# A hand-written side queue for two attentions: its clock, its rotations and its banks

## The chip, the core and the metric

The kernel runs on one core of a Trainium2 chip. The metric is the device time of one execution in microseconds, lower is better. A run's time is the median of several executions; a profile is taken from one execution more.

## What is computed

Two transformer blocks follow each other on one sequence of 256 tokens and width 1024, in fp32. The change touches the second one, cut here to what matters:

```python
def second_block(x, ...):                       # two layers
    # layer 0: differential attention, 8 heads of 2 x 64, values of 128
    q, k, v = split(rms_norm(h) @ w_qkv)
    q, k = rope(q), rope(k)                     # rotation by position
    p = softmax(causal(q @ k.T * 64 ** -0.5))   # two maps per head
    a = p[:, 0] - lam * p[:, 1]
    h = h + (rms_norm(a @ v, subln_g) * (1 - lambda_init)) @ w_o
    h = h + square(relu(rms_norm(h) @ w_up)) @ w_down
    # layer 1: latent attention, 8 heads, 128 plain and 64 rotated
    c, k_rope = split(rms_norm(h, kv_in_norm_g) @ w_dkv)     # 256 and 64
    k_nope, v = split(rms_norm(c, kv_norm_g) @ w_ukv)
    q_nope, q_rope = split(rms_norm(rms_norm(h) @ w_dq) @ w_uq)
    s = (q_nope @ k_nope.T + rope(q_rope) @ rope(k_rope).T) * 192 ** -0.5
    h = h + (softmax(causal(s)) @ v) @ w_o
    h = h + square(relu(rms_norm(h) @ w_up)) @ w_down
    return rms_norm(h)
```

## The kernel before

All weights come as one stream of units of 128x1024, in an order written out by hand (`stream_plan`). For each unit ScalarE casts a high part (`whi`, L358) and VectorE subtracts it for a low part (`wlo`, L359); five such slots exist, and `feed` casts the next unit as soon as the matmuls of an old one have been issued. Every product with a weight is three matmuls (high by high, low by high, high by low). Each engine runs its queue in program order, waits on semaphores, and the program is written out in Python, so the order of the Python calls is the order in each queue.

PSUM has eight banks: four that rotate (`psum`) and four (`pacc`, called `fix`) that accumulate the wide products. `banks.take()` hands out the next free one, whose next user waits for what freed it. While the attentions run, `fix` joins the rotating four; before the output product starts, `banks.retire(fix)` takes the four back as each comes free.

The attentions run beside a stream of projections. Class `Side` is the queue for this: parts (Python generators) stand in it, `add` enters one with a condition, and `nudge`, called between groups of projection matmuls, moves a clock on and advances at most two parts: an active one that is due, or a new one that may begin. What a part yields is the time until it is due again.

Differential attention: 16 blocks of `qk`, by head a query's block (g = 0) and a key's (g = 8), 24 matmuls each, with a nudge in the middle and one at the end. After a block ScalarE copies it into one of the two `sg` buffers (`roped`, L1469) and POOL multiplies by the cosine (L1470). The rotation (`rope_end`: two fp32 matmuls on TensorE, then L1474 and L1480, or L1474 and L1478 for a key, on VectorE) is a part of the side queue. `diff_head` is a head in four steps: masks and scores, row maxima (`softmax_exp`, L1189, VectorE), exponentials (L1194, ScalarE), normalising (L1529 to L1537, VectorE); transposes (L1167); product with the values, its squares, POOL's power and the scaling (L1551, VectorE); transposes (L1558) and the high and low part for the next product (`chunk_parts`, L585 and L586). A head may start when its query and key are `ripe`: rotated, and at least 2 of the queue's clock old. `rows_times` then multiplies the heads' outputs by `o_a`, with a nudge every half unit.

Latent attention: after the feed-forward part, `cross.finish` turns the rows and casts units, `cross.norms` and two diagonals follow, then the low-rank units run in the order `dkv` (2), `dq` (4), `dkr`, `ukn` (2), `ukv` (2), `uq` (5). `low_norm` normalises the latent rows (L534, POOL's power, L542), `turn` transposes them on TensorE (L562) and `part_scaled` writes their parts. The copies of the keys are L1303 and L1304. The loop over `UQ_ORDER` makes a rotated query block for two heads and then the two heads' plain query blocks, three products each, and `latent_head` is a head in three steps, beside it.

Of the kernel before, what the change touches and what calls it, by code (L numbers as in the profile page):

```python
# [108 lines left out]
class Lane:  # L109


    def __init__(self, engine, sem):
        self.engine, self.sem = engine, sem
        self.count, self.seen = 0, {}
# [63 lines left out]
class Side:  # L178


    def __init__(self, width, gap=2):
        self.width, self.gap, self.now = width, gap, 0
        self.waiting, self.active = [], []
# [5 lines left out]
    def advance(self, part):  # L189

        gap = next(part, self)
        if gap is not self:
            self.active.append((self.now + (gap or self.gap), part))
            self.active.sort(key=lambda entry: entry[0])

    def soon(self, part):

        self.active.insert(0, (self.now + 1, part))

# [8 lines left out]

    def nudge(self):

        self.now += 1
        for _ in range(2):
            if self.active and self.active[0][0] <= self.now:
                self.advance(self.active.pop(0)[1])
            elif len(self.active) >= self.width or not self.begin():
                return
# [11 lines left out]
def build(nc, stream, x, c_row, cols, const, g_post, rel, lam, final_g, out):  # L228
    plan = stream_plan()
    with ExitStack() as ctx:  # L230
# [1109 lines left out]
        born = {}  # L1340

        def ripe(*js):
            return all(j in t_q and side.now - born[j] >= 2 for j in js)

# [171 lines left out]
        def diff_head(hh):  # L1516
# [22 lines left out]
            rooms.give(x1, *ts)  # L1539
            yield 4  # L1540
            pt, t = transpose_p(x0, ts)
            yield
            b, tk = times_v(pt, [vd[:, i, P * hh:P * hh + P] for i in range(2)], P, t, t_v)
# [10 lines left out]
            rooms.give(ds, t)  # L1554
            yield 4
            b = banks.take()
# [4 lines left out]

        side = Side(5)
        born.clear()
        for hh in range(8):
            side.add(diff_head(hh), lambda hh=hh: ripe(hh, 8 + hh))

        def rope_end(at, rope):
            t_q[at], born[at] = next(rope), side.now
            yield

        for hh in range(8):
            for g in (0, 8):
                if hh == 7:
                    banks.retire(fix if g == 0 else [])
                b = banks.take()
                u = Unit(("qk", g + hh))
                tk = block_T(b.ap[:, 0:T], u, range(8), n1, b.free, side.nudge)
                u.release(tk)
                rope = roped(kT[:, hh, :] if g else qT[:, 2 * hh:2 * hh + 2, :], b, tk, 1.0 if g else 0.125, *by_r)
                next(rope)  # L1580
                feed()
                side.nudge()
                side.soon(rope_end(g + hh, rope))
        while banks.leaving:
            side.step()
        cross = Whole([(n1, lambda c: col("mlp_g", c), None, list)])
        rows_times([("o_a", k) for k in range(8)], range(8), n2, None, cross, side.nudge)
        cross.finish()
# [12 lines left out]
        feed_forward("mlp0_", DFF2 // P, False, n1, cross, norms_later(was))  # L1601
        cross.finish(True, 1)
        cross.norms()
# [5 lines left out]
        feed()  # L1609

        widths_kv, acc_of = {"dkv": (n1, 4, T, 0), "dq": (n2, 2, 384, 2)}, {}

# [16 lines left out]
        for name, f, last in [("dkv", f, 1) for f in range(2)] + [("dq", f, 3) for f in range(4)]:  # L1629
            u = Unit((name, f))  # L1630
            for i in range(2):
                low(name, f, u, i, last)
            u.release(pe.last())
            feed()
            if (name, f) == ("dq", 1):
                by_r = scaled_tables(t_diag, 11264)
            if (name, f) == ("dkv", 1):
                t_ckv = low_norm([acc_of["dkv", i] for i in range(2)], fix[0:2], T, 0)
        done_q = [acc_of["dq", i] for i in range(2)]
        ckv, cq = Parts(hhi, hlo), Parts(mhi, mlo)  # L1640
        part_scaled(turn(tmp[:, :, 0:T], 2, t_ckv), [(ckv, lambda c: col("kv_g", c))])
        t_cq = low_norm(done_q, fix[2:4], 384, 512)
# [10 lines left out]
        for f in range(2):  # L1653
            u = Unit(("ukn", f))
            for g in range(4):
                b = banks.take()
                tk = block_T(b.ap[:, 0:T], u, (2 * g, 2 * g + 1), ckv, b.free)
                n = 4 * f + g
                if n == 1:
                    t_kr = next(rope)  # L1660
                t = copied(kn[:, n, :], b.ap[:, 0:T], n, tk)
                banks.give(b, t)
                t_kn.append(t)
            u.release(tk)
            feed()
# [13 lines left out]
        def latent_head(hh):  # L1679
# [12 lines left out]
            for i in range(2):  # L1692
                a, w = widths(i)
                t = dve.do(lambda e: e.tensor_scalar(ex.ap[:, a:a + w], ex.ap[:, a:a + w], rs[:, i:i + 1], None,
                                                     ALU.mult), t)
            yield 3
            pt, t = transpose_p(ex, t)
            yield
            b = banks.take()
# [6 lines left out]
        o2 = Parts(nhi, nlo)  # L1706
        side = Side(5, 2)
        born.clear()
# [3 lines left out]
        for n, blk in enumerate(UQ_ORDER):  # L1712
# [3 lines left out]
            for k in range(3):  # L1716
                m = 3 * n + k
                if m % 8 == 0:
                    units.append(Unit(("uq", m // 8)))
                u = units[m // 8]  # L1720
                w = (m % 8) * P
                tk = products([(b.ap[:, 0:T], [(u.part(w, w + P), cq.rows(k), cq.t[k])], k == 0, k == 2)],
                              [*u.ready, *b.free])
                if m % 8 == 7 or m == 35:
                    u.release(tk)
                    feed()
                if k == 1:
                    side.nudge()
            if blk < 8:
                born[8 + blk], t_qr[8 + blk] = side.now, []  # L1730
                t_qn[blk] = t = (act.do(lambda e: e.activation(qn[:, blk, :], b.ap[:, 0:T], ACT.Copy, scale=scale), tk)
                                 if blk % 2 else
                                 dve.do(lambda e: e.tensor_scalar(qn[:, blk, :], b.ap[:, 0:T], scale, None, ALU.mult), tk))
                banks.give(b, t)
                if pend is not None:
                    t_qr[pend[0]], born[pend[0]] = next(pend[1]), side.now
                    pend = None
            else:
                rope = roped(qr[:, 2 * (blk - 8):2 * (blk - 8) + 2, :], b, tk, scale)
                next(rope)  # L1740
                pend = (blk - 8, rope)
            side.nudge()
        while banks.leaving:
# [4 lines left out]
        cross = Whole([(n1, lambda c: col("mlp_g", 8 + c), None, list)])  # L1748
        rows_times([("o_b", k) for k in range(8)], range(8), o2, None, cross, side.nudge)
        t_fg = sp.load(fg, bass.AP(tensor=final_g.tensor, offset=final_g.offset, ap=[[0, P], [1, D]]), s_fg, 16,  # L1750
# [143 lines left out]
```

How the kernel before makes its waits and increments, by code:

```python
    def wait(self, *after):  # L116
        for a in after:
            for sem, value in ([a] if isinstance(a, tuple) else a or []):
                if self.seen.get(id(sem), 0) < value:
                    self.seen[id(sem)] = value
                    self.engine.wait_ge(sem, value)
# [1 line left out]
    def do(self, op, *after):  # L124
        self.wait(*after)
        self.count += 1
        op(self.engine).then_inc(self.sem, 1)
        return self.sem, self.count
# [6 lines left out]
    def load(self, out, in_, sem, value, *after):  # L136
        self.wait(*after)
        self.engine.dma_start(out, in_).then_inc(sem, 16)
        return sem, value
```

## Time and profile before

| | us |
|---|---|
| median of 3 runs | 1203.94 (1201.38 to 1204.03) |
| the profiled execution's own time | 1204.62 |
| its span, first to last instruction | 1203.3 |
| TensorE busy with matmuls | 1147.3 (95%) |
| VectorE busy | 804.2 (67%) |
| ScalarE busy | 620.8 (52%) |

A matmul is pipelined, and its end is modelled, so a share of TensorE near 100% does not say that it runs at its peak. The mean granted clock is 0.989 of full speed (2.4 GHz). The differential heads run from about 628 to 711 us of the span, the low-rank stage from 912 to 949, the latent heads from 952 to 1001.

### The profile page before, as it was taken

The numbers are of one execution on the slowest core, as the hardware profiler recorded it, in microseconds if no ns is written. First come the engines' busy times: TensorE is split into PE (matmuls) and PEld (weight loads), VectorE is DVE, ScalarE is ACT, GpSimd is POOL, SyncE is SP. The second block draws the span as 40 slices with busy tenths as digits, with TensorE's granted clock in tenths as the row PEclk, the third lists the DMA queues.
The fourth block names the chain that finished last, engine by engine and source line by source line (L and its number), as shares of the span: only waits on it lengthen the run. The fifth ranks groups of instructions, "written<-read, shape, count | busy, mean of one in ns | idle before, by whom it ended". The sixth has DMA issues, their size and how long they took to land.

```text
span 1203.3 us, 19170 instructions
## 1 busy us (share of the span) xinstructions
PE 1147.3 (95%) x7554; PEld 1049.8 (87%) x7554; DVE 804.2 (67%) x1332; ACT 620.8 (52%) x1138; POOL 51.5 (4%) x71
## 2 busy tenths in 40 slices
PE   4999999899999899999999799999998889999997
PEld 4988899699988899999889789999998778999996
DVE  4878888787765665655778766655657665655655
ACT  5645444646655544444555445545446444645543
POOL 3100000000000000000012100000000100000000
PEclk8999999999999899999999999999999999999999
DMA  8969998373322566564453334555554413655530
GB/s 341 401 261 415 354 338 324 141 284 139 106 76 101 197 213 225 202 230 157 159 180 106 106 105 154 197 178 197 186 178 141 171 36 126 241 178 195 188 140 36
DMA packets 34009, 231.75 MB, mean 193 GB/s; under 512 B 3704, under 2 KB 5120, under 8 KB 6528
## 3 DMA queue, kind: packets, MB, share of 16 engines
q1 hardware_dynamic: 31952, 226.24, 51.4%
q10 hardware_dynamic: 1968, 4.29, 1.0%
q8 instruction: 60, 0.98, 0.3%
q14 instruction: 29, 0.24, 0.1%
HBM read 229.45 MB, written 1.06 MB: 192 GB/s over the span
## 4 chain that ended last, share of the span: by engine, by line
PE 78%; DVE 11%; ACT 7%; issue 2%; DMA 1%; POOL 1%; DVEq 0%; SPq 0%; ACTq 0%; POOLq 0%
PE ps L396 36%; PE pacc L396 33%; DVE wlo L359 4%; ACT whi L358 2%; PE ps L406 2%; PE ps L409 2%; ACT wk L1194 2%; PE pacc L406 1%; ACT arena L675 1%; DVE st L1189 1%; POOL st L525 1%; DMA raw<-in_stream 1%; DMA cst<-in_const 1%; PE pacc L409 1%; DVE raw L336 0%
## 5 line engine op out<-in xcount | busy, mean ns | idle before, releaser
L359 DVE TENSOR_TENSOR wlo<-raw,whi 128x1024 fp32r<-128x1024 f32 x353 | 429.4, 1224 | 169.1 <-ACT whi L358 161.6
L358 ACT ACTIVATE whi<-raw 128x1024 fp32r<-128x1024 f32 x353 | 368.5, 1055 | 153.7 <-PE pacc L396 74.3
L396 PE MATMUL ps<-nhi,whi 128*128 128x256 f32 x1256 | 363.8, 290 | 3.3 <-DVE arena L1474 1.8
L396 PE MATMUL ps<-nlo,whi 128*128 128x256 f32 x1256 | 358.1, 285 | 0.0
L396 PE MATMUL ps<-nhi,wlo 128*128 128x256 f32 x1256 | 357.9, 285 | 0.0
L396 PEld LDWEIGHTS ps<-nhi,whi 128*128 128x128 f32 x1256 | 243.3, 194 | 9.2 <-DVE arena L1474 2.0
L396 PEld LDWEIGHTS ps<-nlo,whi 128*128 128x128 f32 x1256 | 243.4, 194 | 4.4 <-issue 0.5
L396 PEld LDWEIGHTS ps<-nhi,wlo 128*128 128x128 f32 x1256 | 243.3, 194 | 0.0
L915 ACT ACTIVATE sg<-ps 128x256 f32<-128x256 f32 x104 | 39.8, 383 | 161.2 <-PE ps L396 161.2
L396 PE MATMUL pacc<-whi,mhi 128*128 128x512 f32 x240 | 95.6, 398 | 0.0
L396 PE MATMUL pacc<-wlo,mhi 128*128 128x512 f32 x240 | 94.0, 392 | 0.0
L396 PE MATMUL pacc<-whi,mlo 128*128 128x512 f32 x240 | 93.5, 390 | 0.0
L917 DVE TENSOR_TENSOR hm<-sg,ps 128x256 f32<-128x256 f32 x104 | 43.7, 420 | 70.7 <-ACT sg L915 70.7
L336 DVE SCALAR_TENSOR_TENSOR raw<-raw,silu_c 128x1024 f32<-128x1024 f32 x72 | 88.2, 1233 | 0.0
L396 PE MATMUL pacc<-whi,hhi 128*128 128x512 f32 x188 | 73.9, 393 | 0.7 <-DVE hm L917 0.7
L396 PE MATMUL pacc<-wlo,hhi 128*128 128x512 f32 x188 | 73.6, 391 | 0.0
L396 PE MATMUL pacc<-whi,hlo 128*128 128x512 f32 x188 | 73.2, 389 | 0.0
L525 POOL TENSOR_TENSOR st<-st,mod 128x1 f32<-128x1 f32 (+1 forms) x36 | 22.7, 631 | 1014.6 <-DVE st L680 598.1
L396 PE MATMUL pacc<-whi,nhi 128*128 128x512 f32 (+1 forms) x128 | 49.6, 388 | 6.8 <-DVE nlo L776 3.4
L396 PEld LDWEIGHTS pacc<-whi,mlo 128*128 128x128 f32 x240 | 45.1, 188 | 9.9
L396 PEld LDWEIGHTS pacc<-whi,mhi 128*128 128x128 f32 x240 | 45.3, 189 | 8.2 <-issue 0.5
L396 PEld LDWEIGHTS pacc<-wlo,mhi 128*128 128x128 f32 x240 | 45.3, 189 | 7.7 <-issue 0.5
(333 smaller groups left out, 1769.9 us busy)
## 6 DMA issues: line engine op xcount, KB each, us to landing
raw<-in_stream SPq DMA_DIRECT2D x213, 1024.0 KB, 4.9
gates<-in_g_post ACTq DMA_DIRECT2D x3, 512.0 KB, 7.2
h<-in_x SPq DMA_DIRECT2D x1, 1024.0 KB, 7.0
cst<-in_const ACTq DMA_DIRECT2D x1, 1024.0 KB, 5.0
arena<-bias_rows ACTq DMA_DIRECT2D x1, 1024.0 KB, 14.0
out<-tmp SPq DMA_DIRECT2D x4, 256.0 KB, 2.2
silu_c<-in_c_row ACTq DMA_DIRECT2D x1, 512.0 KB, 5.7
arena<-in_final_g SPq DMA_DIRECT2D x1, 512.0 KB, 3.4
```

Source lines behind the costliest of these rows:

```text
L336: t = dve.do(lambda e: e.scalar_tensor_tensor(src, src, 1.0, silu_c[:, :], ALU.mult, ALU.mult, accum_out=adac[:, 8 * m + k:8 * m + k + 1]) ...
L358: t_hi = act.do(lambda e: e.activation(whi[:, s, :], src, ACT.Copy), arrived, room)
L359: t_lo = dve.do(lambda e: e.tensor_tensor(wlo[:, s, :], src, whi[:, s, :].bitcast(F32), ALU.subtract), arrived, room, t_hi)
L396: return e.matmul(o, lt[a], rh[b], start=start and first, stop=stop and last)
L406: pe.quiet(lambda e: e.matmul(o, lt, rh, start=start, stop=stop), *after)
L409: return pe.do(lambda e: e.matmul(o, lt, rh, start=start, stop=True), *after)
L525: return pool.do(lambda e: e.tensor_tensor(r, v, ex, ALU.pow), t, t_zero)
L675: return act.do(lambda e: e.activation(junk, src, ACT.Square, scale=D ** -0.5, accum_out=sums[:, f:f + 1]), *after)
L915: t = act.do(lambda e: e.activation(sg[:, m, :], up if gate is None else gate, ACT.Relu if gate is None else ACT.Silu), tk)
L917: t = dve.do(lambda e: e.tensor_tensor(hm[:, m, :], sg[:, m, :], up, ALU.mult), t)
L1189: t = dve.do(lambda e: e.tensor_reduce(mx[:, i:i + 1], src[:, a:a + w], AX_X, ALU.max, negate=True), t_src)
L1194: toks.append(act.do(lambda e: e.activation(dst.ap[:, a:a + w], src[:, a:a + w], ACT.Exp, bias=mx[:, i:i + 1], accum_out=sm[:, i:i + 1]), ...
```

## The change

- The side queue's clock counts microseconds of stream: a nudge moves it by 1.4 beside a half block (0.72 and 0.36 in the latent loop, where it was 1), and every advanced part adds `cost` = 0.8. The heads' yields change with it: 8, 3 and 5 for 4, 2 and 4 in `diff_head`, 5 and 2.5 for 3 and 2 in `latent_head`. `ripe` asks for 2 there and 2.5 here.
- A rotation is no longer put at the head of the queue with a due time one nudge on, but sorted in with 2.8; and its generator ends at once, where before it stayed for one empty step. In the latent loop the rotation is done after the second product of the second plain block, and no longer after the first plain block.
- At the last differential head the four `fix` banks leave two and two.
- `cross.finish` casts two units ahead of the norms instead of one. The transposes and parts of the latent `ckv` stand after the second `dq` unit, and the tables of the rotation after the third; before, the tables stood after the second and the transposes behind the fourth.
- Two blocks of `ukn` share a bank and one copy.

```diff
@@ class Side
-    def __init__(self, width, gap=2):
+    def __init__(self, width, gap=2, cost=0):
...
         gap = next(part, self)
+        self.now += self.cost
         if gap is not self:
...
-    def soon(self, part):
-        self.active.insert(0, (self.now + 1, part))
+    def soon(self, part, gap):
+        self.active.append((self.now + gap, part))
+        self.active.sort(key=lambda entry: entry[0])
...
-    def nudge(self):
-        self.now += 1
+    def nudge(self, time=1):
+        self.now += time
@@ ripe
+        rest = [2]
         def ripe(*js):
-            return all(j in t_q and side.now - born[j] >= 2 for j in js)
+            return all(j in t_q and side.now - born[j] >= rest[0] for j in js)
@@ diff_head
-            yield 4
+            yield 8
             pt, t = transpose_p(x0, ts)
-            yield
+            yield 3
...
-            yield 4
+            yield 5
@@ the differential loop
-        side = Side(5)
+        side = Side(5, 3, 0.8)
+        def nudge():
+            side.nudge(1.4)
         def rope_end(at, rope):
             t_q[at], born[at] = next(rope), side.now
+            return
             yield
...
                 if hh == 7:
-                    banks.retire(fix if g == 0 else [])
+                    banks.retire(fix[2:4] if g else fix[0:2])
...
-                side.nudge()
-                side.soon(rope_end(g + hh, rope))
+                nudge()
+                side.soon(rope_end(g + hh, rope), 2.8)
@@ the low-rank stage
-        cross.finish(True, 1)
+        cross.finish(True, 2)
...
-            if (name, f) == ("dq", 1):
-                by_r = scaled_tables(t_diag, 11264)
             if (name, f) == ("dkv", 1):
                 t_ckv = low_norm([acc_of["dkv", i] for i in range(2)], fix[0:2], T, 0)
+            if (name, f) == ("dq", 1):
+                part_scaled(turn(tmp[:, :, 0:T], 2, t_ckv), [(ckv, lambda c: col("kv_g", c))])
+            if (name, f) == ("dq", 2):
+                by_r = scaled_tables(t_diag, 11264)
-        part_scaled(turn(tmp[:, :, 0:T], 2, t_ckv), [(ckv, lambda c: col("kv_g", c))])
...
-            for g in range(4):
+            for g in range(2):
                 b = banks.take()
-                tk = block_T(b.ap[:, 0:T], u, (2 * g, 2 * g + 1), ckv, b.free)
+                for c in range(2):
+                    k = 4 * g + 2 * c
+                    tk = block_T(b.ap[:, c * T:(c + 1) * T], u, (k, k + 1), ckv, b.free)
...
-                t = copied(kn[:, n, :], b.ap[:, 0:T], n, tk)
+                t = copied(kn[:, n:n + 2, :], b.ap.rearrange("p (c t) -> p c t", c=2), g, tk)
@@ latent_head
-            yield 3
+            yield 5
             pt, t = transpose_p(ex, t)
-            yield
+            yield 2.5
@@ the latent loop
-        side = Side(5, 2)
+        side = Side(5, 2, 0.8)
+        rest[0] = 2.5
...
                 if k == 1:
-                    side.nudge()
+                    if pend is not None and blk % 2 and blk < 8:
+                        t_qr[pend[0]], born[pend[0]] = next(pend[1]), side.now
+                        pend = None
+                    side.nudge(0.72)
...
-                if pend is not None:
-                    t_qr[pend[0]], born[pend[0]] = next(pend[1]), side.now
-                    pend = None
...
-            side.nudge()
+            side.nudge(0.36)
```

## Rows read from the trace of the kernel before

**Rows 1.** Stages between starts of row maxima (us, each engine's busy, clock, DMA, GB/s).
```profile
631.34:640.39 9.05, 9.05 (x71) 8.84 (x70) 7.65 (x19) 4.76 (x13) 1.86 (x2) 1.00 0.32 118
640.39:651.09 10.70, 10.70 (x84) 10.43 (x83) 8.49 (x23) 5.17 (x17) 2.15 (x3) 1.00 0.30 100
...
662.07:673.12 11.05, 9.97 (x76) 9.23 (x74) 8.85 (x24) 5.53 (x18) 2.12 (x3) 1.00 0.26 95
673.12:684.09 10.97, 9.49 (x69) 8.55 (x67) 8.77 (x24) 5.53 (x18) 2.17 (x3) 1.00 0.27 96
684.09:698.22 14.13, 10.23 (x51) 9.44 (x52) 8.95 (x24) 5.53 (x18) 2.14 (x3) 0.76 0.23 76
698.22:706.21 7.99, 7.99 (x43) 6.62 (x42) 5.88 (x20) 3.77 (x14) 0.69 (x1) 1.00 0.38 131
```

**Rows 2.** VectorE's timeline over one head: start, duration, instruction, idle time before it.
```profile
662.07 1.15 DVE L1189 TENSOR_REDUCE st<-ps 128x1 f32<-128x128 f32 x4
...
664.54 0.17 DVE L1530 RECIPROCAL st<-st 128x2 f32<-128x2 f32 x1 [0.64 <-ACT wk L1194]
...
666.82 0.42 DVE L1474 TENSOR_TENSOR arena<-pacc,arena 128x256 f32<-128x256 f32 x1
...
667.61 1.22 DVE L359 TENSOR_TENSOR wlo<-raw,whi 128x1024 fp32r<-128x1024 f32 x1
668.75 0.48 DVE L586 SCALAR_TENSOR_TENSOR n2lo<-pacc,mod,n2hi 128x256 fp32r<-128x256 f32 x1
...
670.10 0.61 DVE L1551 TENSOR_SCALAR wk<-pacc,st 128x128 f32<-128x128 f32 x2 [0.80 <-POOL st L525]
670.63 0.41 DVE L1474 TENSOR_TENSOR sg<-ps,arena 128x256 f32<-128x256 f32 x1
...
671.98 1.23 DVE L359 TENSOR_TENSOR wlo<-raw,whi 128x1024 fp32r<-128x1024 f32 x1
```

**Rows 3.** Timeline of all engines at one head of the latent attention.
```profile
975.10 0.87 DVE L1480 TENSOR_TENSOR arena<-sg,hm 64x256 f32<-64x256 f32 x2
...
976.12 0.46 PE L406 MATMUL pacc<-arena 128*128 128x128 f32 x2 [0.41 <-DVE arena L1480]
...
977.05 0.62 DVE L1189 TENSOR_REDUCE st<-pacc 128x1 f32<-128x128 f32 x2 [0.62 <-PE pacc L409]
```

**Rows 4.** ScalarE's timeline at one block of the differential attention.
```profile
678.75 0.39 ACT L1469 ACTIVATE sg<-ps 128x256 f32<-128x256 f32 x1 [1.16 <-DVE arena L1478]
679.03 1.05 ACT L358 ACTIVATE whi<-raw 128x1024 fp32r<-128x1024 f32 x1
```

**Rows 5.** Stages with TensorE's waits, same columns as the first group.
```profile
683.57:689.31 5.74, 1.32 (x10) 0.95 (x9) 4.44 (x14) 3.82 (x15) 0.73 (x1) 0.94 0.56 186
689.31:695.44 6.13, 6.13 (x26) 5.95 (x27) 3.88 (x9) 0.00 (x0) 0.69 (x1) 0.50 0.00 1
918.64:943.78 25.14, 20.25 (x138) 19.03 (x137) 19.07 (x35) 16.44 (x33) 4.01 (x7) 1.00 0.60 211
949.33:988.70 39.37, 34.42 (x222) 29.33 (x221) 25.34 (x60) 17.83 (x50) 3.20 (x4) 1.00 0.24 81
```

**Rows 6.** TensorE's timeline, one wait and the last head's scores.
```profile
685.79 0.41 PE L1558 MATMUL ps<-cst,wk 128*128 128x128 f32 x2 [2.22 <-ACT wk L1194]
...
704.31 0.60 PE L409 MATMUL ps<-arena 128*128 128x256 f32 x2
```

**Rows 7.** TensorE's timeline in the low-rank stage, matmuls after a wait.
```profile
919.49 0.41 PE L396 MATMUL pacc<-whi,n2hi 128*128 128x384 f32 x1 [0.69 <-DVE wlo L359]
...
923.09 0.41 PE L396 MATMUL pacc<-whi,n2hi 128*128 128x384 f32 x1 [1.25 <-DVE wlo L359]
...
934.51 0.35 PE L396 MATMUL ps<-hhi,whi 128*128 128x256 f32 x1 [1.13 <-DVE hlo L586]
...
938.98 0.39 PE L396 MATMUL ps<-hhi,whi 128*128 128x256 f32 x1 [1.60 <-DVE arena L1304]
```

**Rows 8.** VectorE's timeline in the low-rank stage, the normalised latents.
```profile
928.29 0.48 DVE L542 TENSOR_SCALAR tmp<-pacc,st 128x256 f32<-128x256 f32 x1 [0.66 <-POOL st L525]
```

More of the change, by code:

```diff
@@ L178 @@
 class Side:
-    def __init__(self, width, gap=2):
-        self.width, self.gap, self.now = width, gap, 0
+    def __init__(self, width, gap=2, cost=0):
+        self.width, self.gap, self.cost, self.now = width, gap, cost, 0
         self.waiting, self.active = [], []
@@ L1568, in rope_end @@
             t_q[at], born[at] = next(rope), side.now
+            return
             yield
+        rest[0] = 2
         for hh in range(8):
@@ L1573, in build @@
                 if hh == 7:
-                    banks.retire(fix if g == 0 else [])
+                    banks.retire(fix[2:4] if g else fix[0:2])
                 b = banks.take()
                 u = Unit(("qk", g + hh))
-                tk = block_T(b.ap[:, 0:T], u, range(8), n1, b.free, side.nudge)
+                tk = block_T(b.ap[:, 0:T], u, range(8), n1, b.free, nudge)
                 u.release(tk)
@@ L1586, in build @@
         cross = Whole([(n1, lambda c: col("mlp_g", c), None, list)])
-        rows_times([("o_a", k) for k in range(8)], range(8), n2, None, cross, side.nudge)
+        rows_times([("o_a", k) for k in range(8)], range(8), n2, None, cross, nudge)
         cross.finish()
@@ L1609, in build @@
         feed()
+        ckv, cq = Parts(hhi, hlo), Parts(mhi, mlo)
         widths_kv, acc_of = {"dkv": (n1, 4, T, 0), "dq": (n2, 2, 384, 2)}, {}
@@ L1634, in build @@
             feed()
-            if (name, f) == ("dq", 1):
-                by_r = scaled_tables(t_diag, 11264)
             if (name, f) == ("dkv", 1):
                 t_ckv = low_norm([acc_of["dkv", i] for i in range(2)], fix[0:2], T, 0)
+            if (name, f) == ("dq", 1):
+                part_scaled(turn(tmp[:, :, 0:T], 2, t_ckv), [(ckv, lambda c: col("kv_g", c))])
+            if (name, f) == ("dq", 2):
+                by_r = scaled_tables(t_diag, 11264)
         done_q = [acc_of["dq", i] for i in range(2)]
-        ckv, cq = Parts(hhi, hlo), Parts(mhi, mlo)
-        part_scaled(turn(tmp[:, :, 0:T], 2, t_ckv), [(ckv, lambda c: col("kv_g", c))])
         t_cq = low_norm(done_q, fix[2:4], 384, 512)
@@ L1654, in build @@
             u = Unit(("ukn", f))
-            for g in range(4):
+            for g in range(2):
                 b = banks.take()
-                tk = block_T(b.ap[:, 0:T], u, (2 * g, 2 * g + 1), ckv, b.free)
-                n = 4 * f + g
-                if n == 1:
+                for c in range(2):
+                    k = 4 * g + 2 * c
+                    tk = block_T(b.ap[:, c * T:(c + 1) * T], u, (k, k + 1), ckv, b.free)
+                n = 4 * f + 2 * g
+                if n == 0:
                     t_kr = next(rope)
-                t = copied(kn[:, n, :], b.ap[:, 0:T], n, tk)
+                t = copied(kn[:, n:n + 2, :], b.ap.rearrange("p (c t) -> p c t", c=2), g, tk)
                 banks.give(b, t)
-                t_kn.append(t)
+                t_kn += [t, t]
             u.release(tk)
@@ L1748, in build @@
         cross = Whole([(n1, lambda c: col("mlp_g", 8 + c), None, list)])
-        rows_times([("o_b", k) for k in range(8)], range(8), o2, None, cross, side.nudge)
+        rows_times([("o_b", k) for k in range(8)], range(8), o2, None, cross, nudge)
         t_fg = sp.load(fg, bass.AP(tensor=final_g.tensor, offset=final_g.offset, ap=[[0, P], [1, D]]), s_fg, 16,
```

## The prediction

> **What bounds the kernel now.** The page first: TensorE is busy 95% of the span and VectorE 67%, so what a change of order can give back is TensorE's idle time in the stages it touches. The table by heads [rows 1] cuts the differential heads at the moments at which VectorE begins a head's row maxima. Heads 0 and 1 take 9.05 and 10.70 us with TensorE busy throughout; then a head takes 10.97 to 11.05, while TensorE is busy only 9.97 and 9.49 of them; the step from head 5 to head 6 takes 14.13, with TensorE at a mean clock of 0.76. Then VectorE's timeline over one such head [rows 2]: it has no free time between one head's maxima and the next. Its waits are inside a head (0.64 for an exponential, the like once before it, 0.80 for POOL's power), and each is a wait for the instruction just before it, which no reordering of heads fills. So here VectorE's queue, run in program order, sets 11.05 us a head, and TensorE's waits are its shadow.
>
> The stretches with waits [rows 5] give the ceiling. Between 683.57 and 689.31 TensorE does 1.32 us of work in 5.74: all four `fix` banks have been retired and the four left are held by work that VectorE has not reached. It then runs 6.13 us at a granted clock of 0.50, 1.2 GHz. At full pace those 26 matmuls, at the 0.127 us each of a gapless stretch (71 in 9.05, [rows 1]), take 3.3 us: 2.8 lost. In the stage of the low-rank projections TensorE idles 4.9 of 25.14 us, in the latent heads 4.95 of 39.37. With the idle time of the differential heads (1.1, 1.5 and 3.9 in the three windows from 662.07 to 698.22) all that could be won is some 19 us.
>
> **Differential heads.** No instruction is added or removed; steps move. The side queue's clock, stepped nudge by nudge, gives the order. Before, a key's rotation is due one nudge after its block, in the middle of the next one, and its head starts three nudges later. After, head 4's key block ends at clock 44.0, its rotation is due at 46.8, the nudge in the middle of the next block comes at 45.4 and the one at its end at 47.6: so the rotation comes a whole block after its block. The next nudge, half a block on, comes at 49.8 (0.8 for the rotation, 1.4): the key counts as 2.2 old, 2 is enough, and the head starts. So for every head. Both still give one head per two blocks, and the steps inside a head stand about as far apart as before (one nudge fewer between a head's values and its last transposes). What differs is VectorE's order. Before, a key's rotation is followed by two casts, a query's rotation, a low part and a head's scaling before the head that needs it. After, it is the last thing VectorE does before that head's maxima.
>
> VectorE's work for a head, from starts [rows 2]: the head itself 4.75 (662.07 to 666.82), the key's rotation 0.79 (to 667.61), a cast 1.14 (to 668.75), low part and scaling 1.88 (to 670.63), the query's rotation 1.35 (to 671.98), a second cast 1.14 (to 673.12): 11.05. The order after has the same pieces, the key's rotation last. But now the scores on TensorE wait for that rotation, and the maxima wait for the scores. Behind the waiting scores TensorE has the rest of the block, behind the waiting maxima VectorE has everything. The trace of before shows such a hand-over once, in the latent heads [rows 3]: the rotation's last instruction ends at 975.97, the score matmuls that waited for it start at 976.12, and the maxima that wait for them start at 977.05, after 0.62 of idle on VectorE. That is 1.08 us from rotation to maxima, of which nothing can be hidden, as the queue is in order: **+1.1 a head**, a head every 12.15. Bounds: 0 if VectorE were ahead of TensorE at the rotation (excluded by [rows 1, 2] from head 2 on), 1.5 if the softmax's second half also waits. I take 1.1.
>
> The sum, from head 0's maxima (631.34) to head 7's (706.21), 74.87 before. Heads 0 to 1: +1.1, and +1.6 for a buffer: a block's copy on ScalarE takes the `sg` buffer that the rotation two blocks earlier frees, and the cast queues behind it. Before, this shows as 1.16 of idle on ScalarE for VectorE's L1478, then copy and cast [rows 4]; with the rotation later, VectorE itself then waits for that cast, 0.3 + 1.05 + 0.2 for the signals, where before the first heads have scalings or slack to do. Heads 1 to 2: +1.1 (the old 10.70 becomes 11.75). Heads 2 to 5: 3 x 1.1 = +3.3. Heads 5 to 6: 12.15 in place of 14.13, -2.0; the banks now leave two and two, so the fall to half clock goes, but head 6 still waits for bank and rotation. Heads 6 to 7: +3.1 (11.1 in place of 7.99, because head 6 now starts before the last two rotations, which VectorE does in this stretch). Together +8.2. The first head starts half a block and a rotation earlier, but waits for its key's rotation and the cast ahead of it: 1.7 earlier, between 0 and 2.0 (12 matmuls at 0.127, and the rotation). Head 7's maxima: +6.5. Before, TensorE was ahead by then: its scores ended at 704.91 [rows 6] and VectorE came to them 1.3 later; after, it is not: +1.3. What TensorE has left to do afterwards is the same but for one head's transposes, already done: -0.3. **+7.5**, between +4 (the first head's gain in full and hand-overs of 0.8) and +9.5.
>
> **Low-rank stage.** The second cast before the norms (`finish(True, 2)`) removes the wait at 923.09 [rows 7]: -1.4 with the restart. The low part `hlo` is ready in time: -1.4 (the wait of 1.13 at 934.51). Two keys per bank leave no bank wait at 938.98: -1.8 with the restart. Against that, the latent's transposes now stand in TensorE's queue ahead of the third `dq` unit. They need both rows of normalised latents, and VectorE writes the second at 928.29 to 928.77 [rows 8], behind four casts and two powers that keep their place. A `dq` unit takes 919.49 to 921.84 (the wait of 1.25 before 923.09), 2.1 without its tail, so TensorE comes to them at 923.9 and is done with them at 929 instead of soon after: +4.7, with the units `dq` 2 and 3, `dkr` and `ukn` behind it. Sum +0.1; one bank for the three query transposes, copied last, may come 0.6 late: **+0.5**. If that gap takes the clock down as the one at 683.57 did, 2.8 more, of which 0.6 is that bank's: +2.2. I take it at two chances in three, as this gap has less work in it (0.2 in 5.0 us), so +2.7 in the likeliest case; the ends are 0 and +3.
>
> **Latent heads.** The heads now start in pairs, so TensorE changes less often between kinds of matmuls, and the waits for a copied query right behind a rotation go (4.95 in all, [rows 5]). But the four banks still leave together here, and two heads in flight then share what is left: a head's scores wait for the exponentials of the one before, a pair's first scores for a rotation behind another pair's softmax on VectorE. By the same bookkeeping some 2 us go at head 2 (its query's rotation behind two softmaxes on VectorE), 2.5 at head 0's values (the copied query that frees their bank is behind two more) and 1 at head 5: about 5.5 where there were 5. What is left is the fewer changes between kinds of matmuls, some 15 at about 0.15, an estimate from the first matmul after a wait, which shows 0.39 at 938.98 [rows 7], as long as three of a gapless stream. **-2**, between -5 (every wait gone) and +3.
>
> **How the numbers follow.** 7.5 + 2.7 - 2 = +8.2 on the profiled execution's own 1204.62 us (span 1203.3 and 1.3 around it): 1212.8. The median of the runs shown is 0.7 lower, 1203.94, and the profiled one stands at their upper edge, so 1212. Within 0.3% (3.6 us) is what a measurement of this kernel can't tell from no change.
>
> **Rivals.** *A: the hand-over, as summed*, 1206 to 1218, chance 0.62. *B: TensorE stays the bound.* The steps are spaced so that every rotation finds its copy and every head its bank; then a head costs TensorE's 9.97, the gap at 683.57 and the slow clock go (4.4 and 2.8) and the waits of the last two full heads (1.1 and 1.5): -9.8, with the later stages at -2 to +0.5 some 1194. It decides if VectorE has time left before a key's rotation; for it speaks only that heads 0 and 1 took 9.05 and 10.70, gapless on TensorE; against it [rows 2]. Chance 0.15. The Trainium skill ("Perfetto Trace Analysis", "Identifying the Most-Contended Engine") takes the engine with the highest occupancy for the bottleneck, for TensorE by its weight loads. In the window from 662.07 [rows 1] that is 9.23 of 11.05 against VectorE's 8.85, so by that rule B would hold; the waits inside VectorE's queue, which occupancy leaves out, are why I don't follow it here. *C: both half true*, the hand-over's 1.1 a head paid for by the vanished end stall and latent waits: 1201 to 1206, 1204, chance 0.13. *D: worse*, when TensorE's idle 2 us before each head's scores lower its clock again and again, at 2.8 each for four heads: 1223. For it, the fall at 689.31; against it, that the 2.22 us of idle before 685.79 [rows 6] did not do so by itself. Chance 0.10.
>
> Slower than 0.3%: most of A and D, 0.70. Faster: B and little else, 0.16. Same: the rest, 0.14. Range: 1198 to 1218 leaves out B's core and D.
>
> **What would show it.** In the profile after: about 12.1 us from maxima to maxima in the middle heads; idle on VectorE of about 0.8 before each first row maximum, for TensorE; TensorE's longest waits at the scores, for L1478's line; no wait left at the rotations' matmuls; TensorE idle nearly 5 us at the two latent chunks' transposes, for the scaling in `normed`, and perhaps a clock of 0.5 right after. I am wrong if heads come every 11.0 or less, or if VectorE has idle time ahead of its rotations.

## The result, and the profile after

The kernel after takes 1215.72 us (median of 4 executions, 1212.75 to 1217.24) against 1203.72 before: a ratio of 1.0096 with a 95% interval of 1.0083 to 1.0108, so slower by about 12 us. The profiled execution took 1212.75, the lowest of the four; one more profile of the same kernel, taken among the experiments, took 1217.22, and both are read here.

In the kernel after, lines stand two to four further down: the casts are L360 and L361, the rotations L1478 with L1482 (key) or L1484 (query), the row maxima L1191, the exponentials L1196, the scaling L1555, the matmul helpers L398, L408 and L411, the latent's transposes L564, and `normed` L536 and L544.

The page's first part says little: work and shares are those of before, the span has grown.

```profile
span 1211.4 us, 19176 instructions
...
PE 1145.9 (95%) x7554; PEld 1050.6 (87%) x7554; DVE 803.7 (66%) x1330; ACT 621.3 (51%) x1136; POOL 51.9 (4%) x71
```

The differential heads, cut at the starts of the row maxima as in [rows 1] (us, each engine's busy, clock, DMA, GB/s):

```profile
628.25:640.05 11.80, 8.49 (x64) 7.98 (x63) 7.88 (x18) 4.27 (x12) 1.50 (x2) 1.00 0.26 91
640.05:652.59 12.54, 11.37 (x76) 10.71 (x75) 8.21 (x21) 5.92 (x18) 2.15 (x3) 0.86 0.24 85
652.59:665.15 12.56, 10.07 (x75) 9.44 (x74) 9.00 (x23) 5.64 (x18) 2.16 (x3) 0.96 0.24 85
...
677.75:689.90 12.15, 9.71 (x75) 9.16 (x74) 8.96 (x23) 5.64 (x18) 2.17 (x3) 1.00 0.25 86
689.90:701.99 12.09, 10.01 (x75) 9.19 (x74) 8.96 (x22) 5.64 (x18) 2.15 (x3) 0.99 0.26 89
701.99:713.38 11.39, 11.23 (x58) 9.73 (x58) 8.71 (x23) 5.70 (x17) 1.43 (x2) 0.86 0.25 92
```

Where the clock stayed up, a head comes every 12.15 and 12.09, where it came every 10.97 to 11.05. VectorE's busy time is nearly the same (8.96 for 8.77 to 8.85). What is new is seen on VectorE's timeline over one such head, which answers to [rows 2]:

```profile
675.81 0.41 DVE L1478 TENSOR_TENSOR arena<-ps,arena 128x256 f32<-128x256 f32 x1
676.25 0.42 DVE L1482 TENSOR_TENSOR arena<-arena,hm 128x256 f32<-128x256 f32 x1
677.75 0.62 DVE L1191 TENSOR_REDUCE st<-pacc 128x1 f32<-128x128 f32 x2 [1.08 <-PE pacc L411]
...
679.42 0.17 DVE L1533 RECIPROCAL st<-st 128x2 f32<-128x2 f32 x1 [0.39 <-ACT wk L1196]
680.23 0.17 DVE L1534 RECIPROCAL st<-st 128x2 f32<-128x2 f32 x1 [0.64 <-ACT wk L1196]
...
686.28 0.61 DVE L1555 TENSOR_SCALAR wk<-ps,st 128x128 f32<-128x128 f32 x2 [0.81 <-POOL st L527]
686.81 1.22 DVE L361 TENSOR_TENSOR wlo<-raw,whi 128x1024 fp32r<-128x1024 f32 x1
687.94 0.42 DVE L1478 TENSOR_TENSOR arena<-ps,arena 128x256 f32<-128x256 f32 x1
688.39 0.42 DVE L1482 TENSOR_TENSOR arena<-arena,hm 128x256 f32<-128x256 f32 x1
689.90 0.62 DVE L1191 TENSOR_REDUCE st<-ps 128x1 f32<-128x128 f32 x2 [1.08 <-PE ps L411]
```

The key's rotation (L1482) is now the last thing before the maxima, and the maxima wait 1.08 for the scores. The other waits inside the head, 0.39, 0.64 and 0.81, are for the same instructions as before. Head 7 of the same profile shows the other order: a cast stands between its key's rotation and its maxima, and they don't wait at all.

```profile
711.90 0.42 DVE L1482 TENSOR_TENSOR arena<-arena,hm 128x256 f32<-128x256 f32 x1
712.24 1.22 DVE L361 TENSOR_TENSOR wlo<-raw,whi 128x1024 fp32r<-128x1024 f32 x1
713.38 0.91 DVE L1191 TENSOR_REDUCE st<-ps 128x1 f32<-128x128 f32 x3
```
 TensorE's list of waits from 560 to 745, cut to its first three, shows the same hand-over from its side; the columns are the instruction that waited, what it waited for, the sum in us, how many and the longest:

```profile
PE ps L408 <- DVE arena L1482: 8.4, 5, 3.3
PE pacc L408 <- DVE arena L1482: 6.5, 3, 2.5
PE pacc L398 <- DVE n2lo L588: 1.2, 1, 1.2
```

Fifteen microseconds of scores wait for rotations, eight times. The waits at the rotations' own matmuls (L409 for L1469 before) are gone.

Now the three stages, from marker to marker: the heads from the first low part of the value rows to the first low part for the feed-forward product; the low-rank stage from the first `dq` matmul to the first `ukv` matmul; the latent heads from the first `uq` matmul to the first matmul of the last feed-forward part. Before, then after, then the second profile of after:

```profile
590.28:728.55 138.27, 128.98 (x803) 115.44 (x804) 101.86 (x226) 68.91 (x186) 19.04 (x26) 0.98 0.35 122
919.49:943.78 24.29, 20.09 (x136) 19.00 (x137) 18.22 (x34) 15.59 (x30) 4.01 (x7) 1.00 0.62 218
949.33:1016.92 67.59, 62.06 (x357) 52.17 (x356) 39.44 (x83) 28.89 (x73) 3.20 (x4) 1.00 0.27 95
```

```profile
588.69:737.23 148.54, 130.51 (x803) 116.47 (x804) 102.59 (x226) 70.11 (x186) 18.93 (x26) 0.97 0.32 114
928.17:954.10 25.93, 21.21 (x137) 20.36 (x137) 18.19 (x32) 15.28 (x31) 4.01 (x7) 0.93 0.59 205
959.65:1025.02 65.37, 59.88 (x358) 52.42 (x356) 38.24 (x83) 28.74 (x72) 3.65 (x4) 1.00 0.28 98
```

```profile
590.94:740.07 149.13, 130.88 (x803) 116.44 (x804) 102.87 (x226) 70.15 (x186) 18.97 (x26) 0.97 0.33 113
930.99:957.84 26.85, 22.39 (x137) 21.37 (x137) 18.19 (x32) 15.28 (x31) 4.00 (x7) 0.87 0.55 198
963.39:1029.48 66.09, 61.56 (x358) 53.73 (x356) 38.34 (x83) 28.75 (x72) 3.65 (x4) 0.97 0.28 97
```

In the first profile the stages are worth +10.27, +1.64 and -2.22, +9.7 together; the span grew by 8.1 only because the untouched part ahead of the heads happened to be 1.6 shorter (first marker at 588.69 for 590.28). In the second they are +10.86, +2.56 and -1.50, +11.9 together, close to the 12.0 between the medians. The part ahead of the heads is the same code in all kernels here, and its end wanders between 588.6 and 593.5 with the clock falls in it (at 230 to 270 and 350 to 410), so effects of a few us are read from the stages.

### The profile page after: what moved, and what is told of

Its sections match the earlier page's. It is cut to its first block, busy times and chain, and to the rows that moved or that the text cites. A ratio compares the mean times of both kernels' runs of the same rounds, so it can differ in the third digit from the quotient of the medians.

```text
span 1211.4 us, 19176 instructions
## 1 busy us (share of the span) xinstructions
PE 1145.9 (95%) x7554; PEld 1050.6 (87%) x7554; DVE 803.7 (66%) x1330; ACT 621.3 (51%) x1136; POOL 51.9 (4%) x71
## 4 chain that ended last, share of the span: by engine, by line
PE 75%; DVE 13%; ACT 7%; issue 2%; DMA 1%; POOL 1%; DVEq 0%; ACTq 0%; SPq 0%; POOLq 0%
PE ps L398 35%; PE pacc L398 33%; DVE wlo L361 3%; ACT whi L360 2%; PE ps L408 2%; ACT wk L1196 2%; PE ps L411 1%; PE pacc L408 1%; ACT arena L677 1%; POOL st L527 1%; DVE st L1191 1%; DVE arena L1484 1%; DMA raw<-in_stream 1%; DMA cst<-in_const 1%; DVE raw L338 0%
## 5 line engine op out<-in xcount | busy, mean ns | idle before, releaser
L361 DVE TENSOR_TENSOR wlo<-raw,whi 128x1024 fp32r<-128x1024 f32 x353 | 429.5, 1225 | 170.2 <-ACT whi L360 165.7
L360 ACT ACTIVATE whi<-raw 128x1024 fp32r<-128x1024 f32 x353 | 368.5, 1055 | 156.0 <-PE pacc L398 77.3
L398 PE MATMUL ps<-nhi,whi 128*128 128x256 f32 x1256 | 362.8, 289 | 1.4 <-DVE nlo L778 0.5
L398 PE MATMUL ps<-nhi,wlo 128*128 128x256 f32 x1256 | 356.7, 284 | 0.0
L398 PE MATMUL ps<-nlo,whi 128*128 128x256 f32 x1256 | 356.7, 284 | 0.0
L398 PEld LDWEIGHTS ps<-nhi,whi 128*128 128x128 f32 x1256 | 242.3, 193 | 7.2 <-DVE nlo L588 0.9
L398 PEld LDWEIGHTS ps<-nlo,whi 128*128 128x128 f32 x1256 | 242.4, 193 | 4.4 <-issue 0.5
L398 PEld LDWEIGHTS ps<-nhi,wlo 128*128 128x128 f32 x1256 | 242.0, 193 | 0.0
L398 PE MATMUL pacc<-whi,mhi 128*128 128x512 f32 x240 | 95.5, 398 | 0.0
L398 PE MATMUL pacc<-wlo,mhi 128*128 128x512 f32 x240 | 94.1, 392 | 0.0
L398 PE MATMUL pacc<-whi,mlo 128*128 128x512 f32 x240 | 93.5, 390 | 0.0
L398 PE MATMUL pacc<-whi,hhi 128*128 128x512 f32 x188 | 73.9, 393 | 0.7 <-DVE hm L919 0.7
L398 PE MATMUL pacc<-wlo,hhi 128*128 128x512 f32 x188 | 73.6, 391 | 0.0
L398 PE MATMUL pacc<-whi,hlo 128*128 128x512 f32 x188 | 73.2, 389 | 0.0
L398 PE MATMUL pacc<-whi,nhi 128*128 128x512 f32 (+1 forms) x128 | 49.7, 389 | 6.8 <-DVE nlo L778 3.4
L398 PEld LDWEIGHTS pacc<-whi,mlo 128*128 128x128 f32 x240 | 45.1, 188 | 9.8
L398 PEld LDWEIGHTS pacc<-whi,mhi 128*128 128x128 f32 x240 | 45.3, 189 | 8.3 <-issue 0.5
L398 PEld LDWEIGHTS pacc<-wlo,mhi 128*128 128x128 f32 x240 | 45.3, 189 | 7.7 <-issue 0.5
```

What stands on the lines that cost most here:

```text
L360: t_hi = act.do(lambda e: e.activation(whi[:, s, :], src, ACT.Copy), arrived, room)
L361: t_lo = dve.do(lambda e: e.tensor_tensor(wlo[:, s, :], src, whi[:, s, :].bitcast(F32), ALU.subtract), arrived, room, t_hi)
L398: return e.matmul(o, lt[a], rh[b], start=start and first, stop=stop and last)
```

## The experiments

The theory: VectorE's queue runs in order, the rotation comes last before the maxima that need it, and rotation, scores, maxima in a row cost 1.1 a head. The rivals: the new spacing of the steps or the banks costs the time; or the low-rank stage's gap with the clock behind it does. Each kernel is compared with the kernel before on the same chip. Stage lengths are worked out from the same markers as above:

| kernel | median us | ratio to before (95%) | heads | low-rank | latent |
|---|---|---|---|---|---|
| before | 1203.6 to 1204.0 | | 138.27 | 24.29 | 67.59 |
| after | 1215.72 | 1.0096 (1.0083 to 1.0108) | 148.54 | 25.93 | 65.37 |
| after, again | 1215.51 | 1.0100 (1.0085 to 1.0115) | 149.13 | 26.85 | 66.09 |
| heads' part only | 1216.31 | 1.0106 (1.0093 to 1.0119) | 148.84 | 24.30 | 67.60 |
| late rotation only | 1215.23 | 1.0092 (1.0078 to 1.0105) | 149.29 | 24.29 | 67.56 |
| after, later head | 1209.46 | 1.0055 (1.0040 to 1.0069) | 147.22 | 25.94 | 65.39 |
| after, early rotation | 1205.26 | 1.0011 (1.0002 to 1.0020) | 140.02 | 26.34 | 65.39 |
| pairs of banks only | 1203.74 | 0.9997 (0.9987 to 1.0007) | 138.17 | 24.31 | 67.78 |
| low-rank part only | 1206.53 | 1.0029 (1.0020 to 1.0039) | 138.06 | 26.78 | 67.60 |
| no early transposes | 1202.36 | 0.9989 (0.9980 to 0.9998) | 137.28 | 22.50 | 67.59 |
| latent part only | 1206.16 | 1.0021 (1.0010 to 1.0032) | 138.10 | 24.32 | 67.88 |
| keys and latent | 1203.61 | 0.9997 (0.9989 to 1.0006) | 137.45 | 22.50 | 69.60 |
| low-rank and latent | 1208.60 | 1.0038 (1.0025 to 1.0051) | 138.04 | 26.88 | 69.78 |
| repaired | 1202.95 | 0.9994 (0.9986 to 1.0003) | 139.04 | 22.50 | 66.06 |

**Heads' part only.** Before, with the change's hunks of `Side`, `ripe`, `diff_head` and the differential loop.

```diff
-        side = Side(5)
+        side = Side(5, 3, 0.8)
...
-                side.soon(rope_end(g + hh, rope))
+                side.soon(rope_end(g + hh, rope), 2.8)
```

> The kernel before with only the differential heads' part of the change (clock in us, yields 8/3/5, rotations due 2.8 later, banks leaving in pairs); low-rank and latent stages as before. Hand-over theory: the whole loss sits here, +10 against before (the profiles of before and after differ by 10.3 from the first cast of this stage to its end), 1212 to 1216, a head every 12.1 or more. Rival, the loss sits in the low-rank stage's gap and the clock after it: +3 or less here, 1207 at most.

A loss as large as the whole one is in this part: the heads' stage is 10.6 longer, the other two as before, and the time is longer by 12.8, just above the range. The rival that puts it into the low-rank gap falls.

**Late rotation only.** Before, with its old clock, yields and banks; a rotation is due two nudges after its block, sorted in, and a head may start one nudge after its key's.

```diff
-        self.active.insert(0, (self.now + 1, part))
+        self.active.append((self.now + gap, part))
+        self.active.sort(key=lambda entry: entry[0])
...
+            return
             yield
+        rest[0] = 1
...
-                side.soon(rope_end(g + hh, rope))
+                side.soon(rope_end(g + hh, rope), 2)
```

> The kernel before, old clock and old yields, with only the rotation made late: due 2 nudges after its block and a head may start 1 nudge after its key's rotation, so that the rotation stands right before its head's maxima in VectorE's queue as after the change. Hand-over theory: this alone makes heads come every 12.1 or more, with 1.08 of idle before the maxima: +8 to +11 in the heads' stage, 1211 to 1215. Rival, yields and clock in us carry the loss: +3 or less.

The late rotation alone, which brings the order of rotation and maxima with it, makes the loss: 11.0 in the stage, 11.2 in the time. VectorE's timeline has the same wait (here L1481 is the key's rotation, L1190 the maxima):

```profile
664.86 0.42 DVE L1481 TENSOR_TENSOR arena<-arena,hm 128x256 f32<-128x256 f32 x1
666.36 0.62 DVE L1190 TENSOR_REDUCE st<-pacc 128x1 f32<-128x128 f32 x2 [1.08 <-PE pacc L410]
```

**After, later head.** After, with one number changed.

```diff
-        rest[0] = 2
+        rest[0] = 3.2
```

> The kernel after with one number changed: a head's query and key must be 3.2 of the queue's clock old instead of 2, so that a head starts half a block later, with a cast and the next query's rotation between its key's rotation and its maxima in VectorE's queue. Hand-over theory: 1.1 a head come back for heads 1 to 5, a head every 11.0 to 11.1, no idle before the maxima; less about 2 for heads 6 and 7, which now start behind the last rotation: -5 against after, 1210 to 1211, range -3 to -8. Rival, the loss comes from the spacing of the steps or of the banks: within 2 of after.

Heads 3 to 5 come every 10.98 and 11.11 with no idle before the maxima, and 6.3 of the 12 come back, within the range. Heads 2 and 3 are a miss: they come after 13.40 and 12.61, and there the wait has another form, first VectorE's, then ScalarE's timeline:

```profile
649.90 1.22 DVE L361 TENSOR_TENSOR wlo<-raw,whi 128x1024 fp32r<-128x1024 f32 x1 [1.86 <-ACT whi L360]
```

```profile
648.43 0.38 ACT L1473 ACTIVATE sg<-ps 128x256 f32<-128x256 f32 x1 [2.57 <-DVE arena L1484]
648.71 1.05 ACT L360 ACTIVATE whi<-raw 128x1024 fp32r<-128x1024 f32 x1
```

The rotation is still late, so ScalarE's block copy waits 2.57 for its `sg` buffer, the cast waits behind the copy, and VectorE waits for the cast. This profile is the highest of the kernel's six executions, and has some 10 us at half clock behind its last head (0.51 from 723.0 to 733.5); its stage length says less than its median.

**After, early rotation.** After, with two numbers changed: both waits should go.

```diff
-        rest[0] = 2
+        rest[0] = 4
...
-                side.soon(rope_end(g + hh, rope), 2.8)
+                side.soon(rope_end(g + hh, rope), 1.4)
```

> The kernel after with two numbers changed in the differential heads: a rotation is due 1.4 after its block instead of 2.8 (so it runs in the middle of the next block, as before the change), and a head's query and key must be 4 old instead of 2. Clock in us, yields and pairs of banks stay. Hand-over theory: the idle before the maxima and the wait of casts for a copy buffer both go, heads every 11.0 to 11.1 from head 1 on, heads' stage back to that of before or up to 3 shorter: 1204 to 1206, some 10 less than after. Rival, the yields or the clock in us cost something of their own: 1209 or more, like the run with the later head.

Some 10 of the 12 come back, with the yields, the clock in us and the pairs of banks still in. A cast, not the key's rotation, now stands before the maxima, and there is no idle:

```profile
650.39 1.23 DVE L361 TENSOR_TENSOR wlo<-raw,whi 128x1024 fp32r<-128x1024 f32 x1
651.54 0.62 DVE L1191 TENSOR_REDUCE st<-ps 128x1 f32<-128x128 f32 x2
```

Heads come in pairs, 12.25 and 9.34, as three casts fall between two heads and then one; 21.6 for two, where before had 22.0. The heads' stage is still 1.8 longer than before. The time from the last maxima to the stage's end is 2.2 longer (24.59 for 22.34): TensorE waits 2.33 at the last heads' transposes (721.20) for a scaling, and the clock falls there. One step takes 13.22 beside another fall (0.50 from 658.83 to 662.24), where the same step of the last run below, without a fall, takes 12.25.

**Pairs of banks only.** Before, with the retirement of the change.

```diff
-                    banks.retire(fix if g == 0 else [])
+                    banks.retire(fix[2:4] if g else fix[0:2])
```

> The kernel before with only the banks leaving in pairs at the last differential head. VectorE's work from head 5's maxima to head 7's is 15.2 busy and 3.9 of its usual idle in 22.1, so at most 3 can go if the stall and the half clock behind it were what held it: -2, range -3 to 0, with no clock of 0.50 between 689 and 695. Rival, the end stall and slow clock cost their full 7.2 on TensorE's path: -4 or better.

A miss: no gain. From head 5 to head 6 it is now 10.97 in place of 14.13, as meant, but the wait and the half clock only moved on to head 6's masks:

```profile
693.99 0.69 PE L406 MATMUL ps<-causalr,identr 128*128 128x384 f32 x1 [3.20 <-DVE sg L1476]
```

```profile
693.99:700.50 6.51, 6.51 (x19) 5.41 (x20) 4.72 (x14) 1.83 (x8) 0.00 (x0) 0.53 0.45 161
```

From 5 to 7 it takes 20.99 for 22.12, and the stage's end gives the 1.1 back (head 7's maxima to the end marker 23.36, before 22.34).

**Low-rank part only.** Before, with the second cast, the early transposes and two keys per bank.

```diff
-        cross.finish(True, 1)
+        cross.finish(True, 2)
...
+            if (name, f) == ("dq", 1):
+                part_scaled(turn(tmp[:, :, 0:T], 2, t_ckv), [(ckv, lambda c: col("kv_g", c))])
...
-            for g in range(4):
+            for g in range(2):
```

> The kernel before with only the low-rank part of the change (two casts ahead of the norms, the latent's transposes after the second dq unit, two keys per bank). By the trace of after: +1.6 (1205.5), with TensorE idle 3.5 before the transposes and its clock at 0.50 for some 3 us behind them; +0.5 where the clock stays up. Rival, the early transposes cost all of the median's excess: +3 or more.

+2.49 in the stage, and +3.0 in the time: the stage at its dearer end, with TensorE at 0.50 for some 7 us behind the gap. The rival's number, +3, was nearer; the next run shows that the early transposes make it.

**No early transposes.** The same without the second hunk above: the latent is turned behind the fourth `dq` unit.

> The kernel before with the low-rank part but without the early transposes: two casts ahead of the norms and two keys per bank, the latent's transposes behind the fourth dq unit as before. The hlo write on VectorE, behind the same casts, still sets the start of the key units, so of the three waits only that for a bank goes: -1.8 (1201.9), range -3 to 0, against +3.0 with the early transposes. Rival, the casts or the shared bank themselves cost: no gain, 0 to +2.

As expected, -1.79 in the stage and -1.7 in the time. The key units still start when VectorE has written `hlo`; TensorE only waits longer for them, 2.38 where it had waited 1.13 [rows 7]:

```profile
931.62 0.35 PE L396 MATMUL ps<-hhi,whi 128*128 128x256 f32 x1 [2.38 <-DVE hlo L586]
```

So the early transposes alone cost 26.78 - 22.50 = 4.3.

**Latent part only, keys and latent, low-rank and latent.** Three kernels meant to carry the latent part into the kernel before. The line of `advance` that adds `cost` was missing in all three, so that their clock in the latent heads moves with the nudges alone, and not by 0.8 for each step:

```diff
         gap = next(part, self)
-        self.now += self.cost
         if gap is not self:
```

> The kernel before with only the latent heads' part of the change (clock in us, rest 2.5, yields 5 and 2.5, rotation after the second product). By the trace of after: -2.2, 1201.7. Rival, the pairs of heads only move their waits: within 1 of before.

> The kernel before with two casts ahead of the norms, two keys per bank and the latent heads' part; differential heads as before, the latent's transposes behind the fourth dq unit as before. If the latent part gains its 2.2 where the key banks turn as in after, and the other two edits their measured 1.7: -3.9, 1200 (range 1199 to 1201.5). Rival, the latent part only moves its waits and draws a fall of the clock, as in its run alone: -1.5 to +1, 1202.5 to 1205.

> The kernel before with the whole low-rank part and the latent part: the kernel after without its differential heads. If the parts add as in the trace of after (+1.6 to +2.5, and -2.2): within 0.6 of before, 1203.5 to 1204.6. Rival, they add as they did alone (+3.0 and +2.6): 1209.

So none of them tests its expectation. Read as what they are, they say that the latent yields depend on that line: without it the stage takes 67.88, 69.60 and 69.78, with it 65.37 to 66.09 in five profiles (after twice, later head, early rotation, repaired), and with the old loop 67.56 to 67.78 in six. In those three TensorE idles 6.6 to 6.9 in the stage and its clock falls once or twice; in the five it idles 4.5 to 5.5 and the clock falls once at most. How the missing line brings that about was not followed further, and the latent part with its full clock was not run on the kernel before by itself.

**After, again.** The kernel after, unchanged.

> The kernel after, unchanged, for more executions and a second profile. Hand-over theory: heads' stage 10.3 to 10.6 longer than before whatever the execution, low-rank stage 1.6 to 2.5 longer, latent stage 2.2 shorter: 1213.5 to 1216. Rival, something of 3 to 4 that the first profile does not show is in most executions: a stage of the second profile differs from the first by more than 2.

No stage differs by more than 1.0 from the first profile; nothing of 2 or more is hidden.

**Repaired.** After, with the early rotation and without the early transposes.

```diff
-        rest[0] = 2
+        rest[0] = 4
...
-                side.soon(rope_end(g + hh, rope), 2.8)
+                side.soon(rope_end(g + hh, rope), 1.4)
...
-            if (name, f) == ("dq", 1):
-                part_scaled(turn(tmp[:, :, 0:T], 2, t_ckv), [(ckv, lambda c: col("kv_g", c))])
...
+        part_scaled(turn(tmp[:, :, 0:T], 2, t_ckv), [(ckv, lambda c: col("kv_g", c))])
```

> The kernel after with rotations due 1.4 after their block, heads 4 old, and the latent's transposes back behind the fourth dq unit. By the sum of parts: the early rotation's 1205.3 less the 4.2 to 4.7 of the early transposes: 1200.5 to 1201.5, faster than before by 2 to 3. Rival, a wait elsewhere takes the place of the gap before the transposes: 1203 or more.

12.6 less than after, and not told from before: -1.79 and -1.53 in the later stages stand against +0.77 in the heads. The rival's number was nearer, but no new wait stands in the low-rank stage (22.50, as without the early transposes). In the heads' stage the time behind the last maxima is 2.2 longer, as with the early rotation (24.57 for 22.34). Between the profiles of that kernel and of this one the stages differ by -0.98, -3.84 and +0.67, some 4.2 together as the sum had it, while the medians differ by only 2.3; where the other executions lose the rest is not shown.

## Why the prediction held, step by step

**The hand-over** was right in place, cause and size: "1.08 us from rotation to maxima" stands in the trace as 1.08 before the maxima of heads 0, 1, 2, 4 and 5; heads 3 and 6, beside a fall of the clock, have 1.45 and 1.04, and head 7, with the cast between, none. The steps take 12.15 and 12.09 for the forecast 12.15. The idle time named as the sign, 0.8, was too small: all of the 1.08 is idle. The late rotation alone makes it from the old kernel, and the early rotation takes it away again by two numbers. VectorE's queue is the bound; its usual waits stay, and the new one comes on top.

**The buffer of the block copy** was right: heads 0 to 1 take 11.80 (forecast 9.05 + 1.1 + 1.6 = 11.75), with 1.57 of idle on VectorE for a cast. **The first head** came 1.5 earlier after its marker (39.56 for 41.06), forecast 1.7.

**The term that was too small** is the heads' sum, +7.5 forecast and +10.3 and +10.9 measured. The distances between heads 0 and 7 add up to 85.13 where the steps gave 83.1; 0.2 more is in the first head, 0.5 in the end (head 7's maxima to the marker 23.85 for 22.34, +1.5 for +1.0). The step that failed is that no fall of the clock was put into this stage: rival D had it, at 2.8 a fall. Three falls came, in these stretches of the first profile, the fourth row being that of the low-rank stage:

```profile
640.50:643.80 3.30, 3.30 (x16) 3.14 (x15) 1.94 (x9) 2.14 (x9) 0.00 (x0) 0.51 0.01 2
664.30:667.80 3.50, 3.50 (x16) 3.13 (x15) 1.32 (x5) 1.63 (x8) 0.00 (x0) 0.52 0.00 0
701.60:705.90 4.30, 4.30 (x23) 4.07 (x21) 2.20 (x10) 2.10 (x9) 0.00 (x0) 0.60 0.00 0
937.30:940.80 3.50, 3.48 (x12) 3.48 (x13) 3.02 (x4) 0.84 (x2) 0.00 (x0) 0.51 0.77 269
```

They cost less than D's price, as TensorE is not the bound here. What is paid is the hand-over at half clock: head 3's maxima wait 1.45, and their second half 0.66 more.

```profile
665.15 0.62 DVE L1191 TENSOR_REDUCE st<-pacc 128x1 f32<-128x128 f32 x2 [1.45 <-PE pacc L411]
666.43 0.62 DVE L1191 TENSOR_REDUCE st<-pacc 128x1 f32<-128x128 f32 x2 [0.66 <-PE pacc L411]
```

The second profile has one of its falls elsewhere, and so prices it on the same code: heads 3 and 4 come after 12.20 and 12.23 there with the clock up, for 12.56 and 12.60 here, and head 5 after 12.57 with a fall, for 12.15. The heads next to a fall took 12.54, 12.56, 12.60 and 11.39 where 11.8, 12.08, 12.15 and 11.1 were forecast: 2.0 in all, for three falls. So A held, with a cheap form of D in it. The heads' excess is also most of the 3.7 by which the forecast 1212 lies under the median, inside the range.

**The low-rank stage** came out near the forecast sum, with each half of it smaller: that the sum fits is in part luck. Idle time on TensorE went from 4.20 to 4.72 (first profile, 25.93 - 21.21), +0.5, which is the forecast (its own items, +0.1 and a possible 0.6, are set down there as +0.5); the clock added 1.1 there and 2.3 in the second profile, forecast 2.2. The gap is where it was put:

```profile
935.57 0.48 DVE L544 TENSOR_SCALAR tmp<-pacc,st 128x256 f32<-128x256 f32 x1 [0.66 <-POOL st L527]
...
936.11 0.44 PE L564 MATMUL ps<-cst,tmp 128*128 128x128 f32 x2 [3.47 <-DVE st L536]
937.32 0.69 PE L564 MATMUL ps<-cst,tmp 128*128 128x128 f32 x2 [0.78 <-DVE tmp L544]
...
938.13 0.52 PE L398 MATMUL pacc<-wlo,n2hi 128*128 128x384 f32 x1
```

3.47 and 0.78, for the two latents, then matmuls 0.32 apart in place of 0.18. The first wait is put down to L536, but ends as the first latent's scaling (L544, 935.57 to 936.05) does. But the forecast booked 4.6 of savings to the three removed waits apart from the transposes, and alone they save 1.79: the second cast's 1.4 only lengthens the wait for `hlo`, which VectorE sets, and that wait goes only because the transposes come early. Gains on one queue were added up that stand in a row before the same late instruction.

**The latent heads** came out at -2.2 and -1.5, forecast -2, but the reason given is not shown. As forecast, TensorE's idle time is about the same, 5.53 before and 5.49 after, while the same matmuls are busy 2.2 less (62.06, 59.88). But changes from one matmul line to another fall only from 66 to 61, where some 15 fewer were forecast. What halves is the number of waits, from 13 to 6, longer on average; and a matmul right behind a wait adds 0.33 to 0.48 to the busy time, where one adds 0.17 on average (59.88 in 358). The forecast's price per change was itself read behind a wait. Seven waits less at some 0.24 each would be 1.7 of the 2.2, an estimate from these figures; no run separates the two.

**The rivals.** B needed VectorE to have time ahead of a key's rotation; none of the rotations has idle time directly ahead of it. By the Trainium skill ("Perfetto Trace Analysis", "Identifying the Most-Contended Engine") the engine of the highest occupancy is the bottleneck, and TensorE is judged there by its weight loads, among other things. From 677.75 to 689.90 TensorE's weight loads are busy 9.16 and VectorE 8.96, but it is VectorE's chain of work and waits (1.08, 0.39, 0.64 and 0.81) that fills the 12.15, so here the measurement goes against the rule. C's and D's times lie outside the interval.

## What to carry to other kernels

On an engine that runs its queue in order, look at what stands directly before an instruction that needs another engine's answer: if it is the instruction that the answer comes from, the round trip is paid in full each time, and one unrelated instruction between them hid it here (a cast of 1.22 us, for 1.08). A clock in us that spaces steps on one queue says nothing of that order on another; list the order that it makes, engine by engine. Waits that stand in a row before one late instruction are worth what the last of them is worth, and not their sum.

## What was not expected of the hardware

TensorE's clock fell to 0.50 after idle times of very different lengths. In the first profile of after, falls followed waits of 3.31 (to 639.12), 2.49 (to 663.85), and 0.78 with 1.30 (to 699.09 and 701.01), while waits of 2.32 (to 627.32) and 2.44 (to 688.97) were followed by none; in the second profile, a wait of 2.52 was, and one of 2.50 not. So the same code has three falls in this stage in either profile, but not all at the same heads: the length of one wait did not say whether the clock would fall behind it.
